# SSD stage: running sums spread over the partitions by DMA, clipped diagonal exponents on GpSimd, two banks each for z and values

## The reference

```python
dt = jax.nn.softplus(dt_raw + dt_bias)
a = -jnp.exp(a_log)
# per head: A = cumsum(dt * a) over the tokens
# y_t = sum_(s<=t) (C_t . B_s) * exp(A_t - A_s) * (x_s * dt_s)
y = ssd_chunked_scan(xs * dt[..., None], dt * a, bm, cm)
y = y + xs * d_skip[:, None]
y = y.reshape(b, l, D_INNER) * jax.nn.silu(z)
y = rms_norm(y.reshape(b, l, SSD_GROUPS, D_INNER // SSD_GROUPS), norm_g)
```

## Time and profile before

| | before |
|---|---|
| median of 3 runs | 1852.68 us (1850.35 to 1852.8) |
| the profiled execution: its own time | 1853.19 us |
| its span in the profile | 1851.3 us |
| TensorE busy | 1696.1 us (92%) |
| VectorE busy | 1164.7 us (63%) |
| ScalarE busy | 679.8 us (37%) |
| GpSimd busy | 171.8 us (9%) |
| weights from memory | 130 slabs of 1 MB, median 4.8 us from issue to landing |

### The profile page before, as it was taken

The page is one execution under the profiler, slowest core; times in us unless marked ns, Lnnn a source line. Parts: engine busy times, 40 slices in busy tenths (PEclk is TensorE's granted clock), DMA queues, the critical chain, the costliest instruction groups (busy, mean ns, idle before and its releaser), DMA issues.

```text
span 1851.3 us, 19773 instructions
## 1 busy us (share of the span) xinstructions
PE 1696.1 (92%) x7731; PEld 1346.2 (73%) x7731; DVE 1164.7 (63%) x1446; ACT 679.8 (37%) x956; POOL 171.8 (9%) x134
## 2 busy tenths in 40 slices
PE   3949997999999978998999999976999899999998
PEld 2738876888888866886666688865658678888887
DVE  5886675652355465886677774466766587772374
ACT  2313331321132124443877432257871133331131
POOL 0696610000000000000000000000330000000000
PEclk8869998999999999999999999998999999999999
DMA  7544121222222213221111133221002212322232
GB/s 317 190 158 169 59 114 69 82 100 92 91 106 99 92 68 142 83 100 46 46 46 63 51 138 121 91 80 58 1 1 91 91 69 94 112 91 91 95 111 91
DMA packets 25724, 176.25 MB, mean 95 GB/s; under 512 B 2848, under 2 KB 3232, under 8 KB 4896
## 3 DMA queue, kind: packets, MB, share of 16 engines
q1 hardware_dynamic: 21888, 149.66, 22.5%
q0 software_dynamic: 2304, 16.78, 2.5%
q10 hardware_dynamic: 1440, 8.55, 1.1%
HBM read 170.53 MB, written 4.46 MB: 95 GB/s over the span
## 4 chain that ended last, share of the span: by engine, by line
PE 74%; DVE 14%; ACT 6%; issue 2%; DMA 2%; POOL 2%; ACTq 0%; DVEq 0%; SPq 0%; POOLq 0%
PE bank L1370 23%; PE bank L1371 22%; PE bank L1372 22%; DVE w_lo L736 2%; ACT p L342 2%; ACT pt L342 1%; DMA ada_chunk<-ada 1%; DVE p L1117 1%; PE bank L1777 1%; ACT w_hi L342 1%; PE bank L1661 1%; PE bank L1511 1%; PE bank L1493 1%; DVE rs L748 1%; DVE xdt L1078 1%
## 5 line engine op out<-in xcount | busy, mean ns | idle before, releaser
L1370 PE MATMUL bank<-h,w_hi 128*128 128x512 f32 x1216 | 485.0, 399 | 54.1 <-DVE w_lo L736 22.8
L1371 PE MATMUL bank<-h,w_hi 128*128 128x512 f32 x1216 | 477.8, 393 | 0.0
L1372 PE MATMUL bank<-h,w_lo 128*128 128x512 f32 x1216 | 477.6, 393 | 0.0
L342 ACT ACTIVATE w_hi<-raw 128x2048 fp32r<-128x2048 f32 x130 | 249.3, 1917 | 389.0 <-DMA raw<-slabs 386.3
L736 DVE TENSOR_TENSOR w_lo<-raw,w_hi 128x2048 fp32r<-128x2048 f32 x130 | 305.7, 2352 | 56.3 <-ACT w_hi L342 51.7
L1370 PEld LDWEIGHTS bank<-h,w_hi 128*128 128x128 f32 x1216 | 231.7, 191 | 110.4 <-issue 38.8
L1371 PEld LDWEIGHTS bank<-h,w_hi 128*128 128x128 f32 x1216 | 231.5, 190 | 48.9 <-issue 1.0
L1372 PEld LDWEIGHTS bank<-h,w_lo 128*128 128x128 f32 x1216 | 231.1, 190 | 49.0
L1370 PE MATMUL bank<-a_hi,w_hi 128*128 128x512 f32 x432 | 168.8, 391 | 1.9 <-DVE a_lo L742 1.9
L1371 PE MATMUL bank<-a_lo,w_hi 128*128 128x512 f32 x432 | 168.8, 391 | 0.0
L1372 PE MATMUL bank<-a_hi,w_lo 128*128 128x512 f32 x432 | 168.6, 390 | 0.0
(11 more groups left out here) (323 smaller groups left out, 2374.0 us busy)
## 6 DMA issues: line engine op xcount, KB each, us to landing
raw<-slabs SPq DMA_DIRECT2D x130, 1024.0 KB, 4.8
ada_chunk<-ada POOLq DMA_DIRECT2D x16, 1024.0 KB, 5.2
ada_chunk<-ada ACTq DMA_DIRECT2D x8, 1024.0 KB, 20.2
x<-x_in SPq DMA_DIRECT2D x4, 1024.0 KB, 8.7
spill_x<-x SPq DMA_DIRECT2D x1, 2048.0 KB, 6.7
x<-spill_x SPq DMA_DIRECT2D x2, 1024.0 KB, 5.0
out<-x SPq DMA_DIRECT2D x8, 256.0 KB, 2.0
inv<-inv SPq DMA_DIRECT2D x1, 1024.0 KB, 7.8
```

The costliest lines, as they stand in the source:

```text
L342: return act.activation(out, in_, f, **kw)
L1370: pe.matmul(out, w[0], a[0], start=start, stop=False)
L1371: pe.matmul(out, w[0], a[1], start=False, stop=False)
L1372: return pe.matmul(out, w[1], a[0], start=False, stop=stop)
```

## The change

The three matmuls of `running_sums` are gone, with `pick`, `acum_parts` and the DVE operations that made them. SyncE writes the 32 rows of running sums `acum` to DRAM once, and GpSimd loads one row per head back, spread over all 128 partitions, into one of three buffers `along` (256 KB each). GpSimd also computes the exponents of the four diagonal blocks of a head, min(A_t - A_s, 0), into `p2`; the minimum keeps the part above the diagonal finite, and the mask in `sm` zeroes it. ScalarE has three activations per head on the parts off the diagonal, read from `along`, and two in place on the diagonal blocks, two blocks each. The banks that are set free serve as second banks: z alternates between 0 and 3, the values between 6 and 7, and the waits are for the pair before the last instead of the last. The score strip of bank 6 goes to bank 5. The chunk loads of the modulation weights share eight semaphores instead of sixteen.

```diff
-    acum_parts = at("acum_parts", [S], f32r, A + 103 * K)
+    along = at("along", [3, S], f32, 10 * K)
...
+    spill_acum = nc.dram_tensor("spill_acum", (SSD_H, S), f32, kind="Internal").ap()
...
-    group_banks, latent_banks = [banks[n] for n in (2, 3, 4, 7)], [banks[n] for n in (5, 6)]
+    group_banks, latent_banks = [banks[n] for n in (2, 4, 5, 3)], [banks[n] for n in (5, 6)]
...
-        return ((1, 0), (2, 0), (6, 0), (2, 384))[j]
-    near_banks, far_banks = [banks[n] for n in (5, 7)], [banks[n] for n in (3, 4)]
+        return ((1, 0), (2, 0), (5, 0), (2, 384))[j]
+    z_banks, value_banks = [banks[n] for n in (0, 3)], [banks[n] for n in (6, 7)]
...
+                if n == SLAB0["xbc"] + 6:
+                    sp.wait_ge(sem("dt_rows"), 1)
+                    sp.wait_ge(sem("x_spilled"), 32)
+                    sp.dma_start(spill_acum, acum[0:SSD_H, :]).then_inc(sem("x_spilled"), 16)
...
-                do.tell(fn(zt[:], banks[0][:], ACT.Tanh, scale=0.5), "z_tanh", pair + 1)
+                do.tell(fn(zt[:], z_banks[pair % 2][:], ACT.Tanh, scale=0.5), "z_tanh", pair + 1)
             def exponentials(hd):
-                act.wait_ge(sem("bc2_done"), hd + 1)
+                act.wait_ge(sem(f"along_in{hd % 3}"), 16 * (hd // 3) + 16)
                 e2, shift = p2[hd % 4], nac_col[:, :, hd:hd + 1]
-                if hd == 2:
-                    act.wait_ge(sem("x_spilled"), 32)
                 for nth, (j, lo, hi, used) in enumerate(paired(0)):
                     if hd >= 4:
                         act.wait_ge(sem("pv2_done"), TOK * (hd // 2 - 2) + nth + 1)
-                    do(fn(e2[:, used:used + P], near_banks[hd % 2][:, lo:lo + P], ACT.Exp, bias=shift[:, j, :]))
                     if j < TOK - 1:
-                        ins = fn(e2[:, used + P:used + hi - lo], far_banks[hd % 2][:, lo + P:hi], ACT.Exp, bias=shift[:, j, :])
+                        ins = fn(e2[:, used + P:used + hi - lo], along[:, hd % 3, lo + P:hi], ACT.Exp, bias=shift[:, j, :])
                         if nth < TOK - 1:
                             do(ins)
                         else:
-                            do.tell(ins, "e2_made", hd + 1)
+                            do.tell(ins, "far_made", hd + 1)
+                act.wait_ge(sem("near_made"), TOK * (hd + 1))
+                two, two_more = diagonals(e2, 0)
+                do(fn(two, two, ACT.Exp))
+                do.tell(fn(two_more, two_more, ACT.Exp), "e2_made", hd + 1)
...
-            do(dve.memset(pick[:].bitcast(f32), 0.0))
-            do(dve.tensor_copy(pick[0:32, :], ident[0:32, 0:32]))
-            do(dve.tensor_copy(pick[32:64, :], ident[32:64, 32:64]))
...
-            do(dve.memset(acum_parts[:].bitcast(f32), 0.0))
-            do(dve.tensor_copy(acum_parts[0:32, :], acum[0:32, :]))
-            do(dve.tensor_tensor(acum_parts[32:64, :], acum[0:32, :], acum_parts[0:32, :].bitcast(f32), ALU.subtract))
...
-                free(dve.scalar_tensor_tensor(zt[:], zt[:], 1.0, banks[0][:], ALU.add, ALU.mult), "z", pair)
+                free(dve.scalar_tensor_tensor(zt[:], zt[:], 1.0, z_banks[pair % 2][:], ALU.add, ALU.mult), "z", pair)
...
-                do.tell(dve.scalar_tensor_tensor(y, y, col("d_skip", pair), banks[6][:], ALU.mult, ALU.add), "ys_made", pair + 1)
...
+            def along_load(hd):
+                pool.dma_start(along[:, hd % 3, :], spill_acum[hd:hd + 1, :].to_broadcast([P, S]))\
+                    .then_inc(sem(f"along_in{hd % 3}"), 16)
+            pool.wait_ge(sem("x_spilled"), 48)
+            for hd in range(2):
+                along_load(hd)
+            pool.wait_ge(sem("dt_col_ready"), 1)
+            for hd in range(SSD_H):
+                pool.wait_ge(sem(f"along_in{hd % 3}"), 16 * (hd // 3) + 16)
+                if hd >= 4:
+                    pool.wait_ge(sem("pv2_done"), TOK * (hd // 2 - 1))
+                for j, lo, hi, used in paired(0):
+                    pool.tensor_scalar(p2[hd % 4][:, used:used + P], along[:, hd % 3, lo:lo + P], nac_col[:, j, hd:hd + 1], 0.0,
+                                       ALU.add, ALU.min).then_inc(sem("near_made"), 1)
+                if hd + 2 < SSD_H:
+                    if hd:
+                        pool.wait_ge(sem("near_made"), TOK * hd)
+                        pool.wait_ge(sem("far_made"), hd)
+                    along_load(hd + 2)
...
-            def running_sums(hd):
-                if hd >= 2:
-                    pe.wait_ge(sem("e2_made"), hd - 1)
-                picked, near = pick[:, hd:hd + 1].to_broadcast([P, P]), near_banks[hd % 2]
-                pe.matmul(far_banks[hd % 2][:, P:S], picked, acum_parts[:, P:S], start=True, stop=True)
-                pe.matmul(near[:], picked, acum_parts[:], start=True, stop=False)
-                pe.matmul(near[:].rearrange("p (j t) -> p j t", j=TOK), causal16, ident16.unsqueeze(1).to_broadcast([P, TOK, P]),
-                          start=False, stop=True).then_inc(sem("bc2_done"), 1)
             def group_scores(g):
+                if g:
+                    pe.wait_ge(sem("s2_taken"), 2 * g)
...
-                    if g and j == 2:
-                        pe.wait_ge(sem("ys_made"), 4 * g - 1)
-                    elif g and j == 0:
-                        pe.wait_ge(sem("s2_taken"), 2 * g)
...
             def z_tile(pair):
                 slab, m = SLAB0["z"] + pair // 2, pair % 2
                 pe.wait_ge(sem("w_split"), slab + 1)
-                if pair:
-                    pe.wait_ge(sem("bank_free"), FREED["z"] + pair)
+                if pair >= 2:
+                    pe.wait_ge(sem("bank_free"), FREED["z"] + pair - 1)
                 for k in range(KT):
-                    last = three(banks[0][:], weights(slab, KT * m + k), (h_hi[:, k, :], h_lo[:, k, :]), k == 0, k == KT - 1)
+                    last = three(z_banks[pair % 2][:], weights(slab, KT * m + k), (h_hi[:, k, :], h_lo[:, k, :]), k == 0, k == KT - 1)
                 last.then_inc(sem("tile_done"), 1)
...
             def pair_values(pair):
                 pe.wait_ge(sem("p2_made"), 2 * pair + 2)
-                if pair:
-                    pe.wait_ge(sem("ys_made"), pair)
-                pe.wait_ge(sem("s2_taken"), 2 * min((pair + 1) // 4, SSD_G - 1) + 1)
+                if pair >= 2:
+                    pe.wait_ge(sem("ys_made"), pair - 1)
                 for nth, (j, lo, hi, used) in enumerate(paired(0)):
                     for half in range(2):
                         hd = 2 * pair + half
-                        last = pe.matmul(banks[6][64 * half:64 * half + 64, lo:hi],
+                        last = pe.matmul(value_banks[pair % 2][64 * half:64 * half + 64, lo:hi],
                                          xdt[:, j, SSD_P * hd:SSD_P * hd + SSD_P], p2[hd % 4][:, used:used + hi - lo],
                                          start=nth == 0, stop=nth == TOK - 1)
                     last.then_inc(sem("pv2_done"), 1)
             group_scores(0)
...
             group_scores(0)
-            pe.wait_ge(sem("mask_made"), 1)
-            for hd in range(2):
-                running_sums(hd)
             for pair in range(XS_T):
                 z_tile(pair)
-                if pair == 0:
-                    for hd in (2, 3):
-                        running_sums(hd)
                 if pair % 4 == 3 and pair + 1 < XS_T:
                     group_scores(pair // 4 + 1)
                 pair_values(pair)
-                if pair + 2 < XS_T:
-                    for hd in (2 * pair + 4, 2 * pair + 5):
-                        running_sums(hd)
             pe.wait_ge(sem("mean_set"), 1)
             def group_means(groups):
```

More of the change, by code:

```diff
@@ L1088, in gated_pair @@
                 dve.wait_ge(sem("pv2_done"), TOK * (pair + 1))
-                do.tell(dve.scalar_tensor_tensor(y, y, col("d_skip", pair), banks[6][:], ALU.mult, ALU.add), "ys_made", pair + 1)
+                do.tell(dve.scalar_tensor_tensor(y, y, col("d_skip", pair), value_banks[pair % 2][:], ALU.mult, ALU.add),
+                        "ys_made", pair + 1)
                 do.tell(dve.scalar_tensor_tensor(y, zt[:], 0.5, y, ALU.mult, ALU.mult), "z_used", pair + 1)
@@ L1317, in ada_load @@
             def ada_load(n):
-                pool.dma_start(ada_chunk[n][:], ada_d[n, :, :]).then_inc(sem(f"ada_in{n}"), 16)
+                pool.dma_start(ada_chunk[n][:], ada_d[n, :, :]).then_inc(sem(f"ada_in{KT + n % KT}"), 16)
             pool.wait_ge(sem("ada_used"), KT)
@@ L1327, in chunk @@
                 acc = ada_sum[n // KT][:]
-                pool.wait_ge(sem(f"ada_in{n}"), 16)
+                pool.wait_ge(sem(f"ada_in{KT + n % KT}"), 16 * (n // KT))
                 scale = c_act[:, n % KT:n % KT + 1]
```

## The result

| | before | changed |
|---|---|---|
| median of 6 runs, us | 1852.74 (1850.35 to 1854.47) | 1841.24 (1837.56 to 1844.94) |
| ratio | | 0.9931, 95% interval 0.9912 to 0.9949 |
| profiled execution, us | 1853.2 | 1837.56 (span 1835.7) |
| stage: start of the first group scores to start of the last values' last matmul, us | 167.7 | 156.8 |

A forecast was written before the change was run, and what follows sets the result against it. TensorE was taken to bound the SSD stage, VectorE and ScalarE close behind. Stage -29.1, ahead of conv -1.7, port +5 gave -25.8 us: 1853.2 to 1827.4, stated as 1827 us; range 1820 to 1845 at 0.8.

The forecast's parts named there:

- the price of GpSimd's work: SSD stage: four 0.37 us operations and 0.9 us per load, 2.4 us a head, 4.8 of a pair's 8.04 us.
- my rival on the other side: SSD stage: GpSimd, serialised with VectorE's port work, bounds at 10.5 us a pair; 1857 us, under "slower", chance 0.08.
- the port in full: SSD stage rival: GpSimd holds VectorE for whole operations, VectorE bounds at 38.1 us per four pairs; 1837 us, chance 0.24.
- signs of being wrong the first: SSD stage: the prediction is wrong if ScalarE waits for GpSimd more than about a microsecond a pair.
- The slack: Head buffers `p2`: of 13.8 us until values are due, 6.4 and up to 5.2 us are needed, leaving 2.2 us.
- The port, in the direction that I priced: SSD stage: GpSimd holds up VectorE's 19 two-SBUF-input operations, 4.4 us over 16 pairs; taken as 5 us.
- -29.1: SSD stage: ends at 1005.5 instead of 1034.6 us, the most that TensorE's side can give.
- TensorE's rate: SSD stage: without running sums and the z wait, TensorE needs 8.04 us a pair, 34.4 us for four pairs.
- The start: Stage start: ScalarE's first exponentials no longer wait for TensorE's running sums; first values run from 876.0 to 878.3 us.
- ScalarE's prices: SSD stage: five activations a head, all reading SBUF at 0.03 us extra each, 2.65 us a head.
- The loads, 0: SSD stage: 256 KB per head, 7.5 us at worst, issued about 8 us ahead, so no cost.
- The 1.7 us ahead of the conv stage: Before the conv stage: removing the three operations that build `acum_parts` from the chain gives -1.7 us.

The follow-up runs named there:

- mult_mask: Changed kernel with GpSimd's sum and minimum replaced by two multiplications and the next group's score copies put ahead of VectorE's gate; 1824.42 us, ratio 0.9840.
- mask_first: Changed kernel with VectorE's copies of the next group's scores put ahead of the gate at a group's end; 1838.04 us, ratio 0.9928.
- mult_mult: Changed kernel with GpSimd's sum and minimum replaced by two multiplications, leaving out the diagonal exponents; 1831.33 us, ratio 0.9889.

## Why the prediction was wrong

**The step that failed** is the price of GpSimd's work: "The same kind of operation at 128 x 128 took 0.372 us", so "2.4 us a head, 4.8 us a pair". That row is of two multiplications; the new operation has a minimum, and costs 0.70 us before anyone disturbs it. That alone is 0.33 us for each of 32 operations, 10.6 us in four pairs. The second part of the same term is how long VectorE holds GpSimd back. I put it at up to 2.3 us behind a tail; measured, the operation takes 1.05 us in the changed kernel (from 906.86 to 947.85 us), and 0.77 against 0.37 us without the minimum, so 0.35 to 0.40 us for each of 32 operations, 11 to 13 us in four pairs (in `mult_mask`, whose period is shorter, 0.86 against 0.37 us). In `mask_first` GpSimd is occupied for 39.2 us in four pairs, 9.8 us a pair, against the 4.8 us of the forecast and the 8.04 us of TensorE. The mechanism of my rival on the other side (GpSimd as the bound, from 10.5 us a pair) was the one at work, at 10.2 us a pair. That the two numbers are so near is luck: GpSimd's own work is 6.8 us a pair (8 x 0.70 and 2 x 0.59) and not 4.8, and VectorE holds it back for about 3 us and not 5.7. Because the early start and the first four pairs, which ran on the lead, gained 13 us, it ended in a gain. The time, 1841 us, lies where the forecast had "the port in full" (1834 to 1845), but that case has VectorE as the bound. Of the forecast's signs of being wrong the first came true: ScalarE waited for GpSimd for 39.1 us, 2.4 us a pair.

**The slack.** "That leaves 2.2 us" did not hold either. Its 3.9 us for two GpSimd passes and a load are 9.0 us with the measured 1.05 and 0.59 us (8 x 1.05 + 0.6), so 2.9 us are lacking. And it did not count that ScalarE's tanh, and with it gate, copies and multiplications, stand in one line behind its wait for GpSimd. This I named as speaking for the port rival and gave no price. With GpSimd's cheaper operation it costs the difference between `mult_mult` and `mult_mask`: 38.0 - 34.7 = 3.3 us in four pairs, 4.5 us of the stage. Part of it is TensorE's clock after its idle time: in `mult_mult` the values at two of the group ends took 3.90 and 4.07 us.

**How the 13 us are shared.** The forecast stage is 167.7 - 29.1 + 5 = 143.6 us, the measured one 156.8. Without the minimum alone it is 145.9, with the copies moved alone 155.7, with both 141.4. So the minimum explains 10.9 us if it goes first and 14.3 if it goes second, the order 1.1 or 4.5 us; the two limits stand side by side. The last pair makes the 1.1 us look small: in `mask_first` its values ran at a granted clock of 0.58, 1.7 us longer than at full clock, and up to their start the order alone brings 2.8 us.

**The port, in the direction that I priced, was mis-sized.** I gave VectorE 4.4 us of holding in four pairs. Its multiplications took 1.527 us in the mean, against 1.49: 0.03 us each; if all 19 lost as much, 0.6 us. VectorE was not the bound of the changed kernel. With both limits away the stage is 141.4 us, where -29.1 alone gives 138.6: what is left for the port and all else is 2.8 us, not 5. The Trainium skill, "SBUF — State Buffer", Who interferes with whom, has the two engines exclude one another for a whole instruction; the traces agree that somebody waits (1.05 against 0.70 us), but it is nearly always GpSimd's short operation that waits for VectorE's 1.5 us, and not the other way.

**What was right.** TensorE's rate, 8.04 us a pair and 34.4 in four: 8.0 in the first group, and 34.07 us in `mult_mask`. The start: ScalarE's table load began at 847.66 us, before TensorE's first group scores, and the first values 8.2 us behind these (forecast 9.5). ScalarE's prices: 0.618, 0.512 and 0.405 us from `along`, and 0.419 us for 256 columns in place, 0.08 better than I took. The loads, 0: they landed in 3.5 us. The second z bank: no wait of z for the gate in the changed kernel.

**The 1.7 us ahead of the conv stage** did not come whole. The three operations on `acum_parts` are gone, but from the scan that makes `acum` to the first group scores it took 140.15 us before and 139.73 us in the changed kernel, and 139.2 to 139.7 us in the eleven others: 0.4 to 1.0 us less. Whether another wait or the clock takes the rest was not followed.

**What stays open.** Behind the stage the changed kernel's profiled execution is 1.6 us longer than that of before, and those of the other kernels 0 to 5 us. The granted clock goes with it. The stretch that lies 200 to 250 us behind the last values, of the kernel before (817.0 us from the start of the last values' last matmul to the end), of `mult_mask` (817.1 us) and of `mult_mult` (822.2 us):

```profile
1234.20:1284.20 50.00, 37.55 (x220) 31.82 (x218) 34.53 (x62) 39.01 (x65) 0.00 (x0) 0.93 0.17 60
```

```profile
1206.50:1256.50 50.00, 37.49 (x220) 31.77 (x218) 34.61 (x62) 39.03 (x65) 0.00 (x0) 0.93 0.17 59
```

```profile
1206.90:1256.90 50.00, 38.41 (x204) 32.48 (x204) 32.52 (x59) 37.34 (x60) 0.00 (x0) 0.86 0.18 62
```

Whether a stage that ends at another moment moves the clock's falls, or they scatter from one execution to the next, no run here separates. Nor do they explain the spread of the stage's start, 857.4 to 867.0 us, which is there already at the scan (718.1 to 727.6 us).

## What to carry to other kernels

Price an operation by a row with the same functions, not only the same engine and shape: here a minimum in place of a multiplication doubled it, and the work moved to a free engine made that engine the bound. Before moving work to another engine, follow what stands in its consumer's queue behind the new wait (here the tanh), since that wait is paid by all of it. And when one cure brings nothing, try it together with the next one: 40.0 us with either half, 35.2 with both.

## What the runs showed of the hardware

- GpSimd, f32, 128 x 128, one scalar from a column: 0.37 us for two multiplications or an addition and a multiplication, 0.71 us as soon as one of the two is a minimum. VectorE did add and minimum in 0.28 us, eight in a row in 1.66 us.
- GpSimd pays for the port, VectorE hardly: beside VectorE's multiplications of 128 x 1280 four clips took 5.17 us instead of 2.8; those multiplications lost 0.03 us each. Beside VectorE operations that read at most one SBUF tensor, a clip kept its 0.71 us (14 cases in the changed kernel).
- After 5.14 us idle, TensorE's 16 matmuls of a pair's values took 4.07 us at a granted clock of 0.58, and 2.37 us at full clock. The length of the idle time alone doesn't decide it: in `mult_mask` 2.12 us idle were followed by 4.07 us at 0.58 (986.81 us), in `mask_first` 2.75 us idle by 2.37 us at full clock (949.72 us).
